# Expert weights in 16 KB runs: a changed layout for the loads of w1, w3 and w2, with the matmul operands rearranged to fit

## The reference

```python
def expert_step(acc, p):
    w1e, w3e, w2e, ge = p                      # 1024x512, 1024x512, 512x1024
    hid = jax.nn.silu(xt @ w1e) * (xt @ w3e)
    return acc + ge[:, None].astype(xt.dtype) * (hid @ w2e), None
```

## Time and profile before

| | |
|---|---|
| median of 3 runs | 1289.3 us (1288.85 to 1289.6) |
| span of the profiled execution | 1289.1 us |
| TensorE busy with matmuls | 935.6 us, 73% |
| its weight loads | 561.1 us, 44% |
| VectorE / ScalarE / GpSimd busy | 360.8 / 303.5 / 46.3 us |
| read from device memory | 441.15 MB |
| mean granted TensorE clock | 0.916 of full speed |

### The profile page before, as it was taken

One profiled execution on the slowest core, in us unless ns is written; L12 is line 12 of the kernel. 1 busy time (PEld: TensorE's weight loads), 2 busy tenths in 40 slices (PEclk: granted clock), 3 DMA queues, 4 the chain that ended last, 5 costly groups with the idle time before them and its releaser, 6 DMA issues.

```text
span 1289.1 us, 25202 instructions
## 1 busy us (share of the span) xinstructions
PE 935.6 (73%) x10245; PEld 561.1 (44%) x10250; DVE 360.8 (28%) x837; ACT 303.5 (24%) x512; POOL 46.3 (4%) x22
## 2 busy tenths in 40 slices
PE   7998897776666666666668998776666666666664
PEld 6976764333323233333337885433333333333332
DVE  4899661111111111111106884111111111111112
ACT  5633541211011011011013754111110110110102
POOL 2144000000000000000000000000000000000000
PEclk9998899998899899899889999999888888888887
DMA  9622298999999999999995478999999999999995
GB/s 339 255 98 99 67 383 320 394 394 394 394 394 394 394 394 394 394 394 394 394 393 208 150 273 331 377 394 394 394 394 394 394 394 394 394 394 394 394 394 196
DMA packets 184146, 442.69 MB, mean 343 GB/s; under 512 B 3680, under 2 KB 4848, under 8 KB 183984
## 3 DMA queue, kind: packets, MB, share of 16 engines
q1 hardware_dynamic: 183696, 440.90, 91.1%
q10 hardware_dynamic: 288, 1.05, 0.2%
q0 software_dynamic: 128, 0.26, 0.1%
HBM read 441.15 MB, written 1.05 MB: 343 GB/s over the span
## 4 chain that ended last, share of the span: by engine, by line
SPq 54%; PE 20%; DVE 10%; DMA 7%; issue 4%; ACT 4%; POOL 0%; DVEq 0%; ACTq 0%
SPq L447 32%; SPq L452 20%; DMA weights<-in_moe_w_dram 7%; PE bank L928 4%; PE bank L599 3%; PE bank L601 3%; PE bank L600 3%; PE bank L940 2%; SPq L437 2%; DVE weights L1434 2%; DVE weights L1411 1%; DVE weights L1425 1%; ACT weights L984 1%; PE bank L949 1%; PE bank L912 1%
## 5 line engine op out<-in xcount | busy, mean ns | idle before, releaser
L928 PE MATMUL bank<-weights,gates 128*32 128x256 f32 x4096 | 312.9, 473 | 179.7 <-DMA weights<-in_moe_w_dram 171.4
L928 PEld LDWEIGHTS bank<-weights,gates 128*32 128x32 f32 x4096 | 156.1, 135 | 320.9 <-DMA weights<-in_moe_w_dram 168.2
L1634 DVE TENSOR_TENSOR gates<-gates,bank 128x128 f32<-128x128 f32 x64 | 18.4, 288 | 487.3 <-ACT gates L984 487.3
L940 PE MATMUL bank<-weights,gates 128*32 128x256 f32 x2048 | 123.8, 382 | 29.4 <-DVE gates L1636 26.1
L984 ACT ACTIVATE gates<-bank 128x128 f32<-128x128 f32 (+1 forms) x68 | 19.9, 296 | 481.2 <-PE bank L928 480.5
L1630 DVE TENSOR_TENSOR gates<-bank,vecs 128x256 f32<-128x256 f32 x64 | 27.2, 425 | 252.1 <-PE bank L921 252.1
L949 PE MATMUL bank<-gates 32*128 32x256 f32 x1024 | 73.3, 400 | 31.2 <-ACT gates L1194 31.2
L940 PEld LDWEIGHTS bank<-weights,gates 128*32 128x32 f32 x2048 | 62.1, 109 | 72.5 <-issue 34.4
L912 PE MATMUL bank<-tok,gates 128*32 128x256 f32 x1024 | 68.5, 385 | 15.6 <-issue 9.8
L949 PEld LDWEIGHTS bank<-gates 32*128 32x128 f32 x1024 | 46.2, 184 | 63.4 <-ACT gates L1194 62.0
L1194 ACT COPY gates<-bank 128x256 f32<-128x256 f32 x64 | 23.8, 372 | 202.2 <-PE bank L940 202.2
(11 more groups left out here) (214 smaller groups left out, 1087.9 us busy)
## 6 DMA issues: line engine op xcount, KB each, us to landing
weights<-in_moe_w_dram SPq DMA_DIRECT2D x188, 2048.0 KB, 19.5
weights<-in_even_w_in_dram SPq DMA_DIRECT2D x6, 2048.0 KB, 14.4
weights<-in_odd_w_in_dram SPq DMA_DIRECT2D x5, 2048.0 KB, 18.8
weights<-in_moe_w_dram SPq DMA_DIRECT2D x8, 1024.0 KB, 10.1
weights<-in_even_w_in_dram SPq DMA_DIRECT2D x2, 1024.0 KB, 10.5
weights<-in_even_w_out_dram SPq DMA_DIRECT2D x1, 2048.0 KB, 8.8
weights<-in_even_w_out_dram SPq DMA_DIRECT2D x2, 1024.0 KB, 4.8
weights<-in_odd_w_out_dram SPq DMA_DIRECT2D x1, 2048.0 KB, 7.6
```

The source lines that it names most:

```text
L928: ins = pe.matmul(bank[6][PASS * j:PASS * (j + 1), 0:T], got_T[:, k % 2, k // 2, :], up[:, k, :, j * P:(j + 1) * P], start=(k == 0), stop= ...
L940: ins = pe.matmul(bank[7][PASS * q:PASS * (q + 1), T:2 * T], hid_T[:, c, :], down[:, c, q * T:(q + 1) * T], start=(c == 0), stop=(c == Q - 1),
```

## The change

The loads of w1 and w3 now go each to a contiguous 4096 floats of the partition (w1 first, then w3), so that both sides of the transfer are contiguous for 16 KB per partition. Of w2 a partition now gets the rows 4p to 4p+3, also 16 KB on both sides. Since row 4p+j of w2 belongs to hidden column 4p+j, quarter j of the w1/w3 matmul must take the columns j, j+4, j+8, ..., and reads every fourth float. The w2 matmul is as before. The two halves in which expert 2 was loaded (half of the chunks of both matrices) become the whole of w3 early and the whole of w1 later; both count on `up_loaded`, and the semaphore `up_early` and the wait for it go.

```diff
-            def up_of(slot):
-                return weights[:, slot, 0:2 * PIECE].rearrange("p (k w f) -> p k w f", k=KC, w=2)
+            def up_of(slot, w):
+                return weights[:, slot, w * PIECE:(w + 1) * PIECE]
 
             def load_up(l, e, slot):
                 for w, src in enumerate((moe_w1, moe_w3)):
-                    sp_q.dma_start(up_of(slot)[:, :, w, :], src[l, bass.ds(e, 1)].rearrange("o (p k) f -> p (o k) f", k=KC)
+                    sp_q.dma_start(up_of(slot, w), src[l, bass.ds(e, 1)].rearrange("o (p k) f -> p (o k f)", k=KC)
                                    ).then_inc(up_loaded[slot], 16)
 
             def load_down(l, e, slot):
-                down = weights[:, slot, 2 * PIECE:].rearrange("p (c d) -> p c d", c=Q)
-                sp_q.dma_start(down, moe_w2[l, bass.ds(e, 1)].rearrange("o (c p) d -> p (o c) d", p=P)
+                sp_q.dma_start(weights[:, slot, 2 * PIECE:], moe_w2[l, bass.ds(e, 1)].rearrange("o (p c) d -> p (o c d)", c=Q)
                                ).then_inc(down_loaded[slot], 16)
 
             def early_up(l):
 
-                for w, src in enumerate((moe_w1, moe_w3)):
-                    sp_q.dma_start(up_of(ORDER[2])[:, KC // 2:, w, :],
-                                   src[l, 2].rearrange("(p k) f -> p k f", k=KC)[:, KC // 2:, :]).then_inc(up_early, 16)
+                sp_q.dma_start(up_of(ORDER[2], 1), moe_w3[l, 2].rearrange("(p k) f -> p (k f)", k=KC)
+                               ).then_inc(up_loaded[ORDER[2]], 16)
...
-                    up = weights[:, slot, 0:2 * PIECE].rearrange("p (k w f) -> p k w f", k=KC, w=2)
+                    up = weights[:, slot, 0:2 * PIECE].rearrange("p (w k f) -> p k w f", w=2, k=KC)
...
                                 ins = pe.matmul(bank[6][PASS * j:PASS * (j + 1), 0:T], got_T[:, k % 2, k // 2, :],
-                                                up[:, k, :, j * P:(j + 1) * P], start=(k == 0), stop=(k == KC - 1),
+                                                up[:, k, :, j:FF:Q], start=(k == 0), stop=(k == KC - 1),
                                                 tile_position=(0, PASS * j), skip_group_check=True)
```

More of the change, by code:

```diff
@@ L282, in rest_is_set @@
             return mine.at(l, len([j for j in range(1, i + 1) if (j in POOL_STEPS[l]) == (i in POOL_STEPS[l])]))
-        up_early = sem("up_early")
         up_loaded = [sem(f"up_loaded_slot{s}") for s in range(SLOTS)]
@@ L466, in first_experts @@
                 sp_q.wait_ge(*step_done.at(l, last_step(l, ("even_out0", "odd_out1")[l])))
-                for w, src in enumerate((moe_w1, moe_w3)):
-                    sp_q.dma_start(up_of(ORDER[2])[:, :KC // 2, w, :],
-                                   src[l, 2].rearrange("(p k) f -> p k f", k=KC)[:, :KC // 2, :]).then_inc(up_loaded[ORDER[2]], 16)
+                sp_q.dma_start(up_of(ORDER[2], 0), moe_w1[l, 2].rearrange("(p k) f -> p (k f)", k=KC)
+                               ).then_inc(up_loaded[ORDER[2]], 16)
                 sp_q.wait_ge(*mix_ready.at(l, 4))
@@ L898, in start @@
                     pe.wait_ge(*normed.at(2 * l + 1, 2))
-                    pe.wait_ge(up_early, 32 * (l + 1))
                     for q in range(Q):
```

## The result

The changed kernel takes 1312.7 us (median of 4 runs, 1310.4 to 1314.5) against 1289.5 us for the kernel before in the same measurement: ratio 1.0175, 95% interval 1.0156 to 1.0193. It is 1.8% slower, where 4.4% faster was forecast, and outside the range.

A forecast was written before the change was run, and what follows sets the result against it. The prediction took the expert weight loads at 394 GB/s as the bound. Faster loads saved 2 x 28.4 = 56.8 us, the strided operand and small edits cost nothing: 1289.3 - 56.8 gives 1232 us, range 1205 to 1300.

The forecast's parts named there:

- What bounds the kernel: Expert loops of both layers: weight loads at 394 GB/s set the pace, 15.965 us an expert against TensorE's 11.59.
- 11.59 + x: TensorE's own period per expert in us, if the w1/w3 matmul group grows by x us over its 3.66.
- the prediction's own line: End of layer 0's last w1/w3 matmul once TensorE sets the pace: 562.3 + 32x us, against 671.8 before.
- The loads: Expert weight loads: 16 KB runs raise 394 to 420 GB/s, 14.98 us an expert, saving 28.4 us a layer.
- The strided operand: w1/w3 matmul reading every fourth float: taken to cost nothing, hidden in the wait for the DMA.
- the room of 2.53: Growth in us of the w1/w3 matmul group that costs nothing: group under 6.2 us, a factor of 1.7.
- break-even of 3.42: Growth in us of the w1/w3 matmul group, to 7.1 us, at which the loads' gain is used up.
- The bound from the nearest rows: Upper bound for the w1/w3 matmul from ScalarE's and VectorE's strided writes: factor 1.77, 6.48 us, kernel at 1251.
- Rival 1: w1/w3 matmul takes one column per four cycles, 7.07 us; loads' gain cancelled, about 1289 us (1275 to 1305); chance 0.2.
- Rival 2: Four side-by-side w1/w3 matmuls share one fetch path by lines: group 13.9 us, kernel about 1723; chance 0.18.
- Rival 3: Loads: run length does not make the rate, which stays at 394 GB/s; 1289 us if the matmul has room; chance 0.07.
- The small edits: Dropping `up_early`, expert 2's loads regrouped, SyncE's pair issues becoming short: each costs nothing.

The follow-up runs named there:

- pairs: Changed kernel, layer 1 reading two neighbours of every eight floats, layer 0's four quarters reading different chunks with a step of four: 1267.0 us, one run.
- the first experiment: Changed kernel with w1 and w3 in 16 KB runs, but w2 in its old 4 KB runs and the w1/w3 matmul on contiguous columns: 1227.0 us, ratio 0.9505.

## Why the prediction was wrong, point by point

**What bounds the kernel.** Right for the kernel before, and the two straight lines that describe a layer, the loads and TensorE's period of 11.59 + x, carry through to the kernels with a step of two, three, four and eight: TensorE's period while it sets the pace is 11.73, 13.63, 15.34 and 15.47 us there, and 11.59 + x gives 11.77, 13.68, 15.36 and 15.50. With the measured x = 3.77 the prediction's own line ends layer 0 at 562.3 + 32 x 3.77 = 682.9, which is 11.1 us later than before; the loop was 10.4 us longer, and 10.5 in layer 1.

**The loads.** Right in kind, and one term of the sum was mis-sized. The rate with 16 KB runs is 428.6 GB/s and not 420. The cost of a run was read too low, 6.4 ns. From the ends (84.5 ns for 2 KB at 388 GB/s, 16384 x 16 / 428.6 = 611.6 ns for 16 KB) it is 75.3 ns for each 2 KB and 9.2 ns for a run. These two numbers are worked out from the ends; the runs between them test them. They put 4 KB runs at 410 GB/s and 8 KB ones at 422, and an expert at 9.79 + 5.11 = 14.90 us with w2 in 4 KB runs and 9.79 + 4.97 = 14.76 with 8 KB runs: measured 14.9 and 14.76. Of the two readings for w2's 4 KB runs, the 407 from the whole period was the better one, and the 402 to 404 of the windows of 4 us was too low; that these windows held slower packets of the transfers beside it is a guess. That rows of more than 8 KB travel whole was right, by the packet count above. At 428.6 GB/s the 180.36 MB of a layer take 420.8 us, so the new loads alone would save 37 us in a layer by this estimate, and not 28.4; the step of two, with w2 in runs of 8 KB, saved 71.5 us in both layers. The Trainium skill, "DMA: Bandwidth & Descriptors", section on the measured bandwidth, has 425 GB/s for 16 MB; the 428.6 here is 1% above it.

**The strided operand: the step that failed.** The prediction took its cost as nothing because "a modest slowdown of the fetch may stay below" the two cycles of a float32 column. The slowdown is not modest: a column in a 16-byte line of its own takes 453/256 = 1.77 ns, 2.07 times the contiguous 218.7/256 = 0.85. The term was put at nothing, and it measured x = 3.77 us, beyond the room of 2.53 and the break-even of 3.42. The bound from the nearest rows, ScalarE's and VectorE's factor of 1.77, was too low as well. Both numbers of each pair hold the instruction's fixed time, which lowers such a factor, but how much of the gap that explains stays open: the extra time for each column is (2026 - 1148)/1024 = 0.86 ns on ScalarE, which added to L928's 0.85 would give the doubling, and (1333 - 753)/1024 = 0.57 ns on VectorE, which would not. These rows of other engines, which write with their step, gave the kind of the effect and not its size.

What the runs show in its place is a price by lines. Two columns on a line: 230 ns between groups with a step of two, 233 with pairs. 1.33 columns: 349 ns. One: 453. At 1.77 ns for each line the 128, 192 and 256 lines of these operands take 227, 340 and 453 ns, and the two times, of the lines and of the array's cycles, do not add up, the longer one holds: at the clock of 0.50 the sum would have been 428 plus what the step adds at full clock, 234, and the spacing was 452. A contiguous operand has 64 lines, 113 ns by this price, well under its 219. With two columns on a line the two times are about equal at full clock.

The Trainium skill, "Advanced Engine Details and Errata", section on SBUF cachelines, asks for at least two hits on a 16-byte line for full performance. For TensorE's moving operand the traces nearly agree: two hits cost 5 to 7% more than contiguous, fewer cost 60% and 107%.

**Rival 1** came nearest and was given 0.2; no more than a chance of 0.25 stood on slower as a whole. It put the price on each reader, which is right, but counted it in cycles of TensorE, four for a column, which is not: at the lower clock the spacing would have had to double, and it stayed at 452 ns. Its 432 ns at full clock, 7.07 us for the group, made it cancel the gain of the loads to the microsecond, and the nearness of 432 to what was measured is luck. The measured 453 ns is 5% more; at 64 us for each microsecond of the group, 7.43 - 7.07 is 23 us, all of what was measured above 1289. Its second sign, TensorE's waits for the DMA gone, came true. Its bounds of 1275 to 1305 were too narrow for that slope: 0.1 us on the group is 6.4 us in the kernel, and beyond the break-even a price needed a wider range.

**Rival 2** is refuted by the runs with one, two and three readers. **Rival 3** is refuted by the first experiment: the run length sets the rate. It does so on either side of the transfer: for w1 and w3 only the runs in SBUF grew, from 2 to 16 KB, for w2 only those in device memory, from 4 to 8 and 16 KB, and each time the rate rose (394, 421, 425, 428 GB/s).

**The small edits** cost nothing that shows; no run has them by themselves. Issues of a pair take 0.8 us, one of the 58 1.06, where they took 9.42 us in the earlier trace rows and up to 11.5 elsewhere in that trace:

```profile
640.21 0.81 SPq L446 DMA_DIRECT2D weights<-in_moe_w_dram  x2
```

## What to carry to other kernels

When a layout is turned for the sake of transfers, look at which operand pays for it in each inner loop, and work out its room first: here 1.7 times the group's time was free, 1.93 the break-even, and 2.03 came (7.43 us over 3.66). Do not go to the end of a trade when the middle has nearly all of it: w2 in 8 KB runs and a step of two floats keep two columns on each line and reach 426 GB/s; w2 in 16 KB runs adds half a percent of rate, and its step of four doubles the matmul. And when a rival's price lies just at the break-even of a steep line, its outcome is open on both sides, and the range must say so.

## What was not expected of the hardware

- Four readers side by side, each fetching a line for every column, are hardly slower than one: 7.38 us with one reader, 7.43 with four, whether or not they walk over the same lines.
- The price of a line, 1.77 ns, is the same at a granted clock of 0.50 and of 1.00 (452 ns for 256 lines at both), where a contiguous operand takes 428 and 219 ns.
- With a step of three, the spacing of 349 ns is 3% above the 340 of the line count. With a step of two it is 230 and with pairs 233 against 227, and with eight 462 against 453. These small differences are measured and not explained.
- One core's loads from device memory held 428 GB/s over 190 us with 16 KB runs (the kernel with the step of three):

```profile
1000.00:1190.00 190.00, 149.22 (x1785) 69.18 (x1777) 24.92 (x92) 28.29 (x61) 0.00 (x0) 0.98 1.01 428
```
